# Hybrid attention block, one core: the softmax sums of the sparse heads taken from ones beside V, and normalised on VectorE

## What is computed

```python
logits = jnp.einsum('bthd,btkd->bhtk', qb, k_sel).astype(jnp.float32) * scale
logits = logits - slopes[None, :, None, None] * dist[:, None]
logits = jnp.where(valid[:, None], logits, -jnp.inf)
p = jax.nn.softmax(logits, axis=-1)
return jnp.einsum('bhtk,btkd->bthd', p.astype(v.dtype), v_sel)
```

## Time and profile before

| what | value |
|---|---|
| median of three runs | 1453.88 us (1454.44, 1453.88, 1448.11) |
| the profiled execution's own time | 1448.33 us |
| its span | 1446.6 us |
| granted TensorE clock, mean of the span | 0.975 |
| busy in the span: PE, DVE, ACT, POOL | 1341.9, 1021.0, 683.7, 722.7 us |

### The profile page before, as it was taken

How to read it: one execution, slowest core, us unless ns; L and a number is a source line. 1 busy time by engine, 2 the same in 40 slices (tenths; PEclk the granted TensorE clock), 3 DMA queues, 4 the chain that set the end, 5 groups by cost and what they waited for, 6 DMA issues and landing times.

```text
span 1446.6 us, 18529 instructions
## 1 busy us (share of the span) xinstructions
PE 1341.9 (93%) x6181; PEld 1071.7 (74%) x6181; DVE 1021.0 (71%) x1464; ACT 683.7 (47%) x1153; POOL 722.7 (50%) x624
## 2 busy tenths in 40 slices
PE   2899999998899999997998899999999999999997
PEld 2668888776566666665876778888888888887886
DVE  4778699988867655553675986666666666368787
ACT  5456677736676655554115633222323234354332
POOL 3134454556677866550002165555555556578552
PEclk9899899998999999998999999999999999999999
DMA  9521244456533344315453244444444445989432
GB/s 326 177 63 30 88 131 130 145 175 189 131 91 100 106 114 118 86 37 197 157 170 117 87 143 163 167 168 167 168 153 145 149 144 197 356 295 327 156 110 117
DMA packets 123562, 220.20 MB, mean 152 GB/s; under 512 B 9386, under 2 KB 52500, under 8 KB 123220
## 3 DMA queue, kind: packets, MB, share of 16 engines
q1 hardware_dynamic: 123476, 219.12, 45.9%
HBM read 160.90 MB, written 57.93 MB: 151 GB/s over the span
## 4 chain that ended last, share of the span: by engine, by line
PE 42%; DVE 7%; issue 2%; DMA 1%; ACT 1%; POOL 0%; DVEq 0%; POOLq 0%; SPq 0%; ACTq 0%
PE ps_out L2288 26%; PE ps_out L2314 12%; PE ps_out L1641 1%; PE ps_out L1625 1%; DVE mod_acc_final L1708 1%; DMA scr_mod_final<-mod_acc_final 1%; DVE y_full L1729 1%; ACT square_junk L2206 0%; DVE x L2550 0%; DVE y_gated L1741 0%; DVE down_part L2548 0%; DVE wgu_lo L2395 0%; PE ps_out L1649 0%; DVE wo_lo_sb L1692 0%; DVE h_sum_t L2362 0%
## 5 line engine op out<-in xcount | busy, mean ns | idle before, releaser
L1985 POOL TENSOR_TENSOR wgu_lo<-wgu_raw,wgu_hi 128x512 fp32r<-128x512 f32 x66 | 97.2, 1481 | 127.6 <-ACT wgu_hi L1977 127.6
L2222 POOL TENSOR_TENSOR dn_lo<-dn_raw,dn_hi 128x512 fp32r<-128x512 f32 x77 | 126.6, 1662 | 67.4 <-ACT dn_hi L2128 67.4
L1977 ACT ACTIVATE wgu_hi<-wgu_sum 128x512 fp32r<-128x512 f32 x88 | 55.2, 632 | 200.0 <-DVE wgu_sum L2378 80.0
L2288 PE MATMUL ps_out<-h_b_t_hi,wgu_hi 128*128 128x512 f32 x352 | 138.3, 393 | 6.7 <-DVE h_b_t_lo L2366 2.6
L2288 PE MATMUL ps_out<-h_b_t_lo,wgu_hi 128*128 128x512 f32 x352 | 137.6, 391 | 0.0
L2288 PE MATMUL ps_out<-h_b_t_hi,wgu_lo 128*128 128x512 f32 x352 | 137.6, 391 | 0.0
L483 POOL TENSOR_TENSOR win_lo<-win_raw,win_hi 128x256 fp32r<-128x256 f32 (+1 forms) x84 | 66.4, 821 | 139.0 <-ACT win_hi L473 115.5
L2128 ACT ACTIVATE dn_hi<-dn_raw 128x1024 fp32r<-128x1024 f32 x77 | 81.2, 1062 | 114.4 <-PE ps_out L2314 55.7
L2314 PE MATMUL ps_out<-dn_hi 128*128 128x512 f32 x308 | 120.4, 391 | 0.0
L2314 PE MATMUL ps_out<-dn_hi,dn_lo 128*128 128x512 f32 x308 | 119.9, 389 | 0.0
L2314 PE MATMUL ps_out<-dn_lo,dn_hi 128*128 128x512 f32 x308 | 119.9, 389 | 0.0
(11 more groups left out here) (346 smaller groups left out, 3650.9 us busy)
## 6 DMA issues: line engine op xcount, KB each, us to landing
scr_act_sums<-act_sums SPq DMA_DIRECT2D x11, 1792.0 KB, 6.9
dn_raw<-scr_act_sums SPq DMA_DIRECT2D x77, 256.0 KB, 5.3
wmod_c<-in_w_mod_dram SPq DMA_DIRECT2D x48, 256.0 KB, 2.9
wgu_raw<-in_w_gate_dram SPq DMA_DIRECT2D x11, 1024.0 KB, 5.5
wgu_raw<-in_w_up_dram SPq DMA_DIRECT2D x11, 1024.0 KB, 5.4
wd_sums<-in_w_down_dram SPq DMA_DIRECT2D x11, 1024.0 KB, 4.8
scr_wd_sums<-wd_sums SPq DMA_DIRECT2D x11, 1024.0 KB, 4.1
dn_raw<-scr_wd_sums SPq DMA_DIRECT2D x44, 256.0 KB, 7.0
```

What stands on the lines that cost most here:

```text
L1985: pool.tensor_tensor(sl[slot(m, x)][:], src, sh[slot(m, x)][:].bitcast(F32), ALU.subtract).then_inc(wlp, 1)
L2222: pool.tensor_tensor(bl[q % NSLOT][:, 1], braw[entry(q)][:, 1], bh[q % NSLOT][:, 1].bitcast(F32), ALU.subtract).then_inc(dlw, 1)
L2288: last = pe.matmul(bank(m, b), a[s][:, t], h[x][t // 2][:, t % 2], start=(fresh and t == 0 and a is sh and h is hh), stop=(t == 3 and a is ...
```

## The change

V's second copy in `vd` becomes ones, so partitions 64 to 127 of `ps_o` hold the sum of the probabilities of each query, the same number on all 64 partitions. The spread goes: its matmuls on PE, its copy on ACT, its bank in the plan, the 128x4 reciprocal on DVE, and the accumulated sums of L1211. In their place DVE evicts all 128 partitions of `ps_o` one step after the group's last transposes (`d_o_raw`, two buffers), and one step later (behind that step's copies) inverts the 64 partitions of sums into `d_sum_reciprocal` and multiplies. PE's next group waits for the eviction (`dev`) instead of for the stored result. The rounding on ACT waits for `onr`, the normalised result.

```diff
-            pool.tensor_copy(g.vd[:, :, HD:P], rl[:, 0].rearrange("p (b d) -> p b d", b=NT)[:, :, HD:P]).then_inc(vdc, 1)
+            pool.memset(g.vd[:, :, HD:P], 1.0).then_inc(vdc, 1)
...
-        return v, [("s", gr) for gr in range(SBG, 2 * SBG) if end.get(gr, -99) == r]
+        return v, []
...
-                p, c = a[gr % 2][:, rows[y][1] % 4, 0:w], 4 * (gr - SBG) + rows[y][1] % 4
+                p = a[gr % 2][:, rows[y][1] % 4, 0:w]
                 act.wait_ge(tt, y - SBR + 1)
-                act.activation(p, p, ACT.Exp, scale=-1.0, bias=nm[:, y - SBR:y - SBR + 1],
-                               accum_out=sm[:, c:c + 1]).then_inc(ex, 1)
+                act.activation(p, p, ACT.Exp, scale=-1.0, bias=nm[:, y - SBR:y - SBR + 1]).then_inc(ex, 1)
...
-            for gr in spread(r):
-                d = gr - SBG
-                lanes = slice(HD * (gr // 2 % 2), HD * (gr // 2 % 2) + HD)
-                act.wait_ge(sd, d + 1)
-                if d >= 4:
-                    act.wait_ge(od, gr - 3)
-                act.activation(spr[lanes, upper(gr)], place(("s", gr))[lanes], ACT.Copy).then_inc(sc, 1)
             for gr in paired(r, 1):
                 stage, pair, G, x, hi, lo = out_parts(gr)
                 n = out_index(gr)
-                act.wait_ge(od, gr + 1)
+                if gr < SBG:
+                    act.wait_ge(od, gr + 1)
+                else:
+                    act.wait_ge(onr, gr - SBG + 1)
...
-            if y >= 5 and r % 4 == 1 and y // 4 <= SBG:
-                d = y // 4 - 1
-                dve.wait_ge(ex, 4 * d + 4)
-                dve.reciprocal(rs[:, 4 * d:4 * d + 4], sm[:, 4 * d:4 * d + 4]).then_inc(rc, 1)
             for gr in ended(r, 1):
-                lanes, G = slice(HD * (gr // 2 % 2), HD * (gr // 2 % 2) + HD), upper(gr)
+                lanes, G = head_lanes(gr), upper(gr)
                 dve.wait_ge(vd, done_by[gr])
+                if gr < SBG:
+                    if gr >= 4:
+                        dve.wait_ge(olr, out_index(gr) - 1)
+                        dve.wait_ge(sqr, out_index(gr) - 1)
+                    dve.tensor_copy(of[lanes, G], o[lanes]).then_inc(od, 1)
+                else:
+                    d = gr - SBG
+                    if d >= 2:
+                        dve.wait_ge(onr, d - 1)
+                    dve.tensor_copy(raw[:, d % 2], o[:]).then_inc(dev, 1)
+            for gr in normalised(r):
+                d = gr - SBG
+                lanes, G = head_lanes(gr), upper(gr)
+                dve.wait_ge(dev, d + 1)
+                if d >= 1:
+                    dve.wait_ge(onr, d)
+                dve.reciprocal(rcp[0:HD], raw[HD:P, d % 2]).then_inc(rcr, 1)
                 if gr >= 4:
                     dve.wait_ge(olr, out_index(gr) - 1)
                     dve.wait_ge(sqr, out_index(gr) - 1)
-                if gr < SBG:
-                    dve.tensor_copy(of[lanes, G], o[lanes]).then_inc(od, 1)
-                else:
-                    dve.wait_ge(sc, gr - SBG + 1)
-                    dve.tensor_tensor(of[lanes, G], o[lanes], spr[lanes, G], ALU.mult).then_inc(od, 1)
+                dve.wait_ge(rcr, d + 1)
+                dve.tensor_tensor(of[lanes, G], raw[0:HD, d % 2], rcp[0:HD], ALU.mult).then_inc(onr, 1)
...
-                    if gr >= 1:
+                    if gr > SBG:
+                        pe.wait_ge(dev, gr - SBG)
+                    elif gr >= 1:
                         pe.wait_ge(od, gr)
...
-            for gr in spread(r):
-                d = gr - SBG
-                await_freed(follows["s", gr])
-                pe.wait_ge(rc, d + 1)
-                for b in range(4):
-                    last = pe.matmul(place(("s", gr))[:, P * b:P * b + P],
-                                     rs[:, 4 * d + b:4 * d + b + 1].to_broadcast([P, P]), g.ident[:],
-                                     start=True, stop=True)
-                last.then_inc(sd, 1)
```

More of the change, by code:

```diff
@@ L1027, in attention @@
     summed = at("tied_summed", [P, SEQ], 108, more=256)
-    nm, sm, rs = (at(name, [P, SBR], 44, more=256 * x) for x, name in enumerate(("neg_max", "prob_sum", "prob_rsum")))
+    nm = at("neg_max", [P, SBR], 44)
     qs = [at("d_q_stack0", [P, SEQ], 64, F32R), at("d_q_stack1", [P, SEQ], 45, F32R)]
@@ L1032, in attention @@
     prod = at("mod_prod_c", [P, HALF], 36)
-    spr = at("rsum_spread", [P, 2, HALF], 51)
+    raw = at("d_o_raw", [P, 2, HALF], 51)
+    rcp = at("d_sum_reciprocal", [P, HALF], 49)
     with ExitStack() as ctx:
@@ L1065, in attention @@
     mad = k.sem("modc_added")
-    rc = k.sem("d_rsum_ready")
-    sd = k.sem("rsum_spread_done")
-    sc = k.sem("rsum_spread_copied")
+    dev = k.sem("d_o_evicted")
+    rcr = k.sem("d_reciprocal_ready")
+    onr = k.sem("d_o_normalised")
     oll = k.sem("oT_lo_last_ready")
@@ L1091, in ended, with head_lanes, normalised @@
         return [gr for gr in end if end[gr] + steps == r]
-    def spread(r):
-        return [gr for gr in end if gr >= SBG and end[gr] == r]
+    def head_lanes(gr):
+        return slice(HD * (gr // 2 % 2), HD * (gr // 2 % 2) + HD)
+    def normalised(r):
+        return [gr for gr in ended(r, 2) if gr >= SBG]
     def paired(r, steps):
@@ L1366, in await_freed @@
                 pe.wait_ge(v_rdy, n + 1)
-            elif kind == "s":
-                pe.wait_ge(sc, n - SBG + 1)
             else:
```

## The result

The changed kernel takes 1476.7 us in the median of four runs (1474.13 to 1479.4), against 1453.56 us for the kernel before (1448.11 to 1454.44). The ratio is 1.0188, with a 95% interval of 1.0157 to 1.0218; the quotient of the two medians, 1.0159, lies at its lower end. I had forecast 1441.3 us, with a range to 1462: the sign was wrong and the time lies outside the range. It is the case that I had called the slow reciprocal.

The account below looks back on a forecast made before the run. PE was taken to bound the sparse stage. 13.1 us off PE's path, less 1.1 on DVE, plus 0.6 at the stage's end gave 12.6 us gain: 1441.3 us on the median, range 1428 to 1462.

Parts of the forecast that it names:

- the slow reciprocal: Rival: each element costs several times a plain one, so the kernel slows to 1471 to 1486 us; nearly all of 0.22.
- PE bounds the stage, and the spread is on its path: Sparse stage: PE sets the pace; removing the spread at step 0 takes 13.1 us off the path.
- the second rival: DVE's chain at step 2 doesn't bind, so step 4's 0.89 us is won too: 19.9 us gain; chance of more gain 0.16.
- The slack on DVE at step 2: New reciprocal and product, 1.43 us ahead of the 640 row, use up step 4's 0.89 us and lose 7 x 0.16 us.
- The reciprocal at 0.69 us: DVE's wide 64x512 reciprocal was taken to run at the plain rate, 0.69 us.
- my own formula: With R the wide reciprocal's time, change of time is -12.6 + 8 x (R - 0.69): seven at step 2, one at the end.
- the point of decision: The wide reciprocal's time at which the gain vanishes: R = 2.27 us, 4.1 ns for each element.
- the far end: Upper estimate of the wide reciprocal, 10 ns for each element: 5.25 us, making the change +24 and up to +32 us.
- the near end: The wide reciprocal at the plain rate, 0.69 us; the forecast gain of 7.3 to 17 us had chance 0.50.
- The product at 0.69 us: DVE's new 64x512 product of two SBUF operands was priced by L1351's 0.688 us.
- The pair at step 6 hidden: DVE's second reciprocal and product, 1.43 us, hide behind PE's long steps 6 to 0, until about 4 us.
- The end of the stage: After the last spread, products end about 0.78 us earlier and the last instruction at 665.7 instead of 666.29: 0.6 us gain.

Follow-up runs that it names:

- e2: Changed kernel without any normalisation: DVE copies the head's 64 partitions straight into o_full, no reciprocal or product; ratio 0.9850 to the kernel before.
- e10: Changed kernel with both POOL's late modulation work cut to 32 columns and four extra matmuls keeping PE busy at step 4; ratio 1.0086 to the kernel before.
- e5: e1 with POOL's modulation products and sums of the late steps cut from 512 to 32 columns; ratio 0.9917 to the kernel before.
- e1: Changed kernel with the wide reciprocal replaced by a copy of the same 64x512; ratio 0.9952 to the kernel before.
- e6: Changed kernel with four extra 128x512 matmuls on PE at the start of step 4 of each head but the first rows; ratio 1.0100 to the kernel before.

## Why the prediction was wrong, step by step

- **PE bounds the stage, and the spread is on its path:** right. e2 gave 21.7 us for it, the second rival's sum 19.9. The step from 557.09 to 558.83 in the earlier trace rows is 1.74 us, and the stage's seven odd-to-even parts fell by 11.2 us in e10 and by 12.1 us in e5 (80.0 after 92.1), where the sum had 6 x 1.74 + 0.89 = 11.3; the seventh 1.74 lies ahead of the first even store, which came 1.8 us earlier.
- **The slack on DVE at step 2:** right. I had said that DVE's chain there uses up the 0.89 us at step 4 and 0.16 us more, so that every further us of the reciprocal counts for seven heads. In e2 the seven even-to-odd parts fell by 6.25 us, which is 7 x 0.89, and in e10, with clock and POOL out of the way, they grew by 20.4 us, 19.7 by the sum.
- **The reciprocal at 0.69 us:** the step that failed. It has 3.35. By my own formula this turns -12.6 into +8.7 us, beyond the point of decision at 2.27 us. That alone would be 1462.6 us, at the upper edge of the range; what follows below took the time to 1476.7. The 168 ns row can't tell the rates apart: I took its excess over other small rows for the price of four elements, with the fixed part of a plain operation. The reciprocal's own fixed part is 0.138 us, shorter than any of the rows beside which I had set it but the one of 128 ns. I had taken a fixed part of about 135 ns as speaking against the slow rate, and it is what the reciprocal has. I had used that 128 ns row for the far end (5.25 us), which does hold the measured time, and then took the near end with a 0.50 chance and gave everything slower 0.22. My estimate of eight plain ticks an element, 4.4 us, pointed the right way, and six is what was measured. It was my reading of the iterative divide with a repeat count of 8 in the Trainium skill, page "VectorE: DVE Perf Modes", section "First, the fixed hardware budget", which states no time.
- **The product at 0.69 us:** wrong beside POOL's work. e1 against e5 puts 5 to 8 us on it and on e1's copy, some 1.5 of them clock; in the changed kernel it is less, 2.4 us of the stage by e6 against e10, within the interval of either ratio. The row that I took, L1351, runs at the end of the stage, where POOL is idle. The stage itself has POOL busy for 16 of 20 us, and I didn't ask what the two share.
- **The clock:** missing from the sum. I had priced a stall by its length. Six of the seven stalls of 3.5 to 4.0 us had a lower clock behind them, which cost 11 us of the stage and 13 us by the ratios (the changed kernel against e6).
- **The pair at step 6 hidden:** nearly right at this length. In e10 that part of the head loses nothing to speak of; in the changed kernel it loses 5 us more (-6.0 where e10 has -11.2), of which 3.3 went with the clock (e6 has -9.3) and 1.9 with POOL.
- **The end of the stage:** undersized. The last head pays both reciprocals, some 3 us more than the formula.

Together for the stage of the changed kernel, in us against before: -12.6 summed; +21.3 for the reciprocal at 3.35; +3.4 for the last head; +2.4 for POOL; +11.1 for the clock. That is +25.6, and the stage measures +26.4. This is no independent check: the last three are read off the runs themselves, and those for POOL and the clock are steps from e10 over e6 to the changed kernel, which must add up. What is tested is the rest: the first two terms give +8.7, and e10 measures +12.9 in the stage and +12 by the ratio. A difference of two ratios has an interval of plus or minus 4 to 6 us.

## What to carry to other kernels

A narrow instruction prices the fixed part of an operation and not its rate: with four elements, the plain rate and six times that rate differ by 21 ns, and the small instructions in the earlier trace rows are spread over 43. Where the rate decides the sign, the range must hold the slow rate and the chances must treat the two as open. Work that moves off the bounding engine lands in somebody's queue, so look for the step at which the new owner has no slack, ask what else uses its way to memory there, and count a stall of TensorE as possibly longer than it is, since the clock behind it may be lower.

## What the runs showed of the hardware that I had not expected

- VectorE's reciprocal of fp32 takes 6.27 ns for each element of a partition's row and 0.14 us fixed (1.743 us at 256, 3.348 at 512), in every one of 32 instances within 5 ns, whatever POOL did.
- A VectorE product of two SBUF operands, 64x512, takes 0.68 us alone and 1.31 to 1.55 us where it starts while POOL's 128x512 work is running (ten products of e1); with one operand in PSUM it takes 0.69 us beside the same work.
- Behind six of seven waits of 3.5 to 4.0 us on PE the granted clock fell (0.67 over the 8 us behind one of them); behind seven waits of 1.5 to 2.1 us it fell once, to 0.79. Extra matmuls inside the wait made the kernel 13 us faster.
- Ln and Exp in turn on ScalarE, from one table set, take 0.63 us each for 64x512.
